# Up projections over 256 tokens as one 512-column and one 256-column matmul per chunk

## What is computed

```python
def swiglu(u, w_gate, w_up, w_down):           # layers 0 and 1, 256 tokens, hidden 2816
    return (jax.nn.silu(u @ w_gate) * (u @ w_up)) @ w_down

def sq_relu_mlp(x, w1, w2):                    # layers 2 (272 tokens) and 3 (256), hidden 4096
    h = jax.nn.relu(x @ w1)
    return (h * h) @ w2
```

## Time and profile before

| | |
|---|---|
| median of 3 runs | 1271.04 us (1270.38 to 1271.95) |
| the profiled execution: time, span | 1271.81 us, 1269.8 us |
| busy: TensorE | 1245.5 us, 98% |
| busy: VectorE, ScalarE, GpSimd | 812.0, 734.6, 365.6 us (64, 58, 29%) |
| L346, L347, L348 on `uhi`, `ulo`: matmuls | 1824 each |
| L362, L363: matmuls | 608 each |
| gu0, gu1, up3: from about | 141.8, 443.5, 1088.8 us |
| dn0, dn1, dn3: from | 264.13, 565.84, 1177.05 us |

### The profile page before, as it was taken

How to read it: one execution, slowest core, us unless ns; L and a number is a source line. 1 busy time by engine, 2 the same in 40 slices (tenths; PEclk the granted TensorE clock), 3 DMA queues, 4 the chain that set the end, 5 groups by cost and what they waited for, 6 DMA issues and landing times.

```text
span 1269.8 us, 26957 instructions
## 1 busy us (share of the span) xinstructions
PE 1245.5 (98%) x9610; PEld 1173.9 (92%) x9610; DVE 812.0 (64%) x1441; ACT 734.6 (58%) x1368; POOL 365.6 (29%) x413
## 2 busy tenths in 40 slices
PE   6999999999999999999999899999999999999998
PEld 6988999998998999998889599999999889999887
DVE  5687755566677655557799975554547766755554
ACT  6476766655455566666566864444346776544433
POOL 2011344421000144441133037770001210678100
PEclk9999999999999999999999899999999999999999
DMA  7542666667665466667655056556555443665764
GB/s 262 182 125 85 195 186 181 185 212 203 206 188 167 135 186 183 193 182 217 183 163 153 6 165 184 178 175 184 172 166 194 146 135 105 194 182 183 199 188 159
DMA packets 65761, 218.68 MB, mean 172 GB/s; under 512 B 9152, under 2 KB 13456, under 8 KB 65552
## 3 DMA queue, kind: packets, MB, share of 16 engines
q1 hardware_dynamic: 63344, 210.99, 54.9%
q10 hardware_dynamic: 2336, 6.58, 1.6%
HBM read 214.04 MB, written 1.08 MB: 169 GB/s over the span
## 4 chain that ended last, share of the span: by engine, by line
PE 76%; issue 10%; DVE 5%; POOL 4%; ACT 3%; DMA 1%; POOLq 0%; SPq 0%; ACTq 0%; DVEq 0%
PE bank L346 19%; PE bank L348 18%; PE bank L347 18%; PE bank L362 8%; PE bank L363 4%; POOL scratch L613 1%; DVE wlo L330 1%; POOL scratch L611 1%; PE bank L960 1%; PE bank L945 1%; POOL ahi_alo L615 1%; PE bank L942 1%; DVE scratch L601 1%; ACT ahi_alo L586 1%; ACT whi L325 1%
## 5 line engine op out<-in xcount | busy, mean ns | idle before, releaser
L330 DVE TENSOR_TENSOR wlo<-raw,whi 128x1024 fp32r<-128x1024 f32 (+1 forms) x391 | 479.7, 1228 | 150.1 <-ACT whi L325 148.3
L346 PE MATMUL bank<-uhi,whi 128*128 128x256 f32 (+1 forms) x1824 | 525.6, 288 | 11.5 <-DVE wlo L330 10.6
L348 PE MATMUL bank<-uhi,wlo 128*128 128x256 f32 (+1 forms) x1824 | 518.0, 284 | 0.0
L347 PE MATMUL bank<-ulo,whi 128*128 128x256 f32 (+1 forms) x1824 | 517.5, 284 | 0.0
L325 ACT ACTIVATE whi<-raw 128x1024 fp32r<-128x1024 f32 (+1 forms) x391 | 407.7, 1045 | 178.6 <-PE bank L363 102.8
L346 PEld LDWEIGHTS bank<-uhi,whi 128*128 128x128 f32 x1824 | 345.4, 189 | 19.8 <-issue 17.1
L348 PEld LDWEIGHTS bank<-uhi,wlo 128*128 128x128 f32 x1824 | 345.6, 189 | 0.0
L347 PEld LDWEIGHTS bank<-ulo,whi 128*128 128x128 f32 x1824 | 344.2, 189 | 0.5
L362 PE MATMUL bank<-ahi_alo,whi 128*128 128x512 f32 x608 | 212.4, 393 | 0.0
L363 PE MATMUL bank<-ahi_alo,wlo 128*128 128x256 f32 x608 | 170.5, 280 | 0.0
L346 PE MATMUL bank<-ahi_alo,whi 128*128 128x272 f32 (+1 forms) x560 | 162.6, 290 | 0.4 <-DVE wlo L330 0.4
(11 more groups left out here) (292 smaller groups left out, 1332.5 us busy)
## 6 DMA issues: line engine op xcount, KB each, us to landing
raw<-stream SPq DMA_DIRECT2D x391, 512.0 KB, 3.9
scratch<-decay ACTq DMA_DIRECT2D x8, 416.0 KB, 4.3
scratch<-relh ACTq DMA_DIRECT2D x8, 384.0 KB, 3.5
scratch<-scratch SPq DMA_DIRECT2D x60, 34.0 KB, 2.6
constants<-consts SPq DMA_DIRECT2D x1, 1300.0 KB, 11.0
h<-xT SPq DMA_DIRECT2D x4, 256.0 KB, 5.4
out<-h SPq DMA_DIRECT2D x8, 128.0 KB, 2.4
scratch<-scratch SPq DMA_DIRECT2D x16, 16.0 KB, 3.2
```

The source lines that it names most:

```text
L330: dve.tensor_tensor(wlo[:, s, 0:w], raw[:, s, 0:w], whi[:, s, 0:w].bitcast(F32), ALU.subtract).then_inc(w_lo, 1)
L346: pe.matmul(dst, hi, a, start=first and i == 0, stop=False)
L347: pe.matmul(dst, hi, b, start=False, stop=False)
L348: mm = pe.matmul(dst, lo, a, start=False, stop=last and i == chunks - 1)
```

## The change

`uhi` and `ulo` become halves of one tensor, so that one access pattern can stream both. In gu0, gu1 and up3 `wide_mm` takes the place of `unit_mm`. The two halves of the bank are then added before anything else: ScalarE copies the second half into a scratch tile (`half_copy`), VectorE adds the first (`half_add`), and the multiply that used to read the bank reads the sum in place. `up2` (272 tokens) stays as it was.

```diff
-        uhi = sb("uhi", DC * T, F32R)[:, :].rearrange("p (c t) -> p c t", t=T)
-        ulo = sb("ulo", DC * T, F32R)[:, :].rearrange("p (c t) -> p c t", t=T)
+        both_u = sb("uhi_ulo", 2 * DC * T, F32R)[:, :].rearrange("p (h c t) -> p h c t", h=2, t=T)
+        uhi, ulo = both_u[:, 0, :, :], both_u[:, 1, :, :]
...
+        half_t = area(V0, 2 * SEQ).rearrange("p (b t) -> p b t", b=2)
...
+                    if wide:
+                        wide_mm(pe, n0 + j, bank[(b0 + j).mod(4)][:, :], both_u, 0, DC, True, True, x)
+                    else:
+                        unit_mm(pe, n0 + j, bank[(b0 + j).mod(4)][:, 0:width(cols)], uhi, ulo, cols, x=x)
...
+        def half_copy(act, n, j, src):
+
+            act.wait_ge(w_used, (n + 1).value())
+            act.activation(half_t[:, j % 2, :], src[:, SEQ:2 * SEQ], ACT.Copy).then_inc(half_copied, 1)
+
+        def half_add(dve, u, j, src, dst):
+
+            dve.wait_ge(half_copied, (u + 1).value())
+            dve.tensor_tensor(dst, src[:, 0:SEQ], half_t[:, j % 2, :], ALU.add).then_inc(half_added, 1)
...
                     split_hi(act, n0 + (2 * j + AHEAD))
+                    half_copy(act, n0 + 2 * j, 2 * j, bank[(b0 + 2 * j).mod(4)])
                     act.wait_ge(evac, (b0 + (2 * j + 1)).value())
...
                     split_hi(act, n0 + (2 * j + 1 + AHEAD))
+                    half_copy(act, n0 + (2 * j + 1), 2 * j + 1, bank[(b0 + 2 * j + 1).mod(4)])
                     act.wait_ge(evac, (b0 + (2 * j + 2)).value())
...
-                    dve.wait_ge(w_used, (n0 + (2 * j + 1)).value())
-                    dve.tensor_tensor(gate[:, j, cols], bank[(b0 + 2 * j).mod(4)][:, 0:width(cols)],
-                                      rstd[:, 0, cols], ALU.mult).then_inc(evac, 1)
+                    half_add(dve, u, 2 * j, bank[(b0 + 2 * j).mod(4)], gate[:, j, cols])
+                    dve.wait_ge(half_added, (u + 1).value())
+                    dve.tensor_tensor(gate[:, j, cols], gate[:, j, cols], rstd[:, 0, cols], ALU.mult).then_inc(evac, 1)
                     split_lo(dve, n0 + (2 * j + AHEAD))
-                    dve.wait_ge(w_used, (n0 + (2 * j + 2)).value())
+                    half_add(dve, u + 1, 2 * j + 1, bank[(b0 + 2 * j + 1).mod(4)], mval[:, j, cols])
+                    dve.wait_ge(half_added, (u + 2).value())
                     dve.wait_ge(t_ready, (i + 1).times(2).value())
-                    dve.tensor_tensor(mval[:, j, cols], bank[(b0 + 2 * j + 1).mod(4)][:, 0:width(cols)],
-                                      tgate[:, j, cols], ALU.mult).then_inc(evac, 1)
+                    dve.tensor_tensor(mval[:, j, cols], mval[:, j, cols], tgate[:, j, cols], ALU.mult).then_inc(evac, 1)
...
+                    if u0 is not None:
+                        u = At(u0 + j, it, 4)
+                        half_add(dve, u, j, src, gate[:, j % 2, cols])
+                        dve.wait_ge(half_added, (u + 1).value())
+                        src = gate[:, j % 2, cols]
+                    dve.scalar_tensor_tensor(out=gate[:, j % 2, cols], in0=src, scalar=0.0,
+                                             in1=rstd[:, 0, cols], op0=ALU.max, op1=ALU.mult).then_inc(evac, 1)
```

More of the change, by code:

```diff
@@ L350, in unit_mm, with wide_mm @@
                 mm.then_inc(w_used, 1)
-        def wide_mm(pe, n, dst, c0, chunks, first, last, x):
+        def wide_mm(pe, n, dst, both, c0, chunks, first, last, x):
             s = n.mod(RING)
@@ L362, in wide_mm @@
                 pe.matmul(dst, hi, both[:, :, c0 + i, FIRST], start=first and i == 0, stop=end, skip_group_check=True)
-                mm = pe.matmul(dst[:, 0:SEQ], lo, ahi[:, c0 + i, FIRST], start=False, stop=end, skip_group_check=True)
+                mm = pe.matmul(dst[:, 0:SEQ], lo, both[:, 0, c0 + i, FIRST], start=False, stop=end, skip_group_check=True)
             mm.then_inc(w_used, 1)
@@ L505, in group @@
                         if wide:
-                            wide_mm(pe, n0 + (j * per + u), bank[(b0 + j).mod(4)][:, :], u * DC, min(DC, kc - u * DC), u == 0, u == per - 1,
+                            wide_mm(pe, n0 + (j * per + u), bank[(b0 + j).mod(4)][:, :], both, u * DC, min(DC, kc - u * DC), u == 0, u == per - 1,
                                     x if wait_x else None)
@@ L548, in resid_dve, with hidden_pe @@
                 split_lo(dve, At(START[name] + DC - 1 + AHEAD))
-        def hidden_pe(pe, name, cols, norm, groups):
+        def hidden_pe(pe, name, cols, norm, groups, wide=False):
             def group(it):
@@ L557, in group @@
                     pe.wait_ge(evac, (b0 + (j - 3)).value())
-                    unit_mm(pe, n0 + j, bank[(b0 + j).mod(4)][:, 0:width(cols)], uhi, ulo, cols,
-                            x=u_chunk(norm) if it is None and j == 0 else None)
+                    x = u_chunk(norm) if it is None and j == 0 else None
+                    if wide:
+                        wide_mm(pe, n0 + j, bank[(b0 + j).mod(4)][:, :], both_u, 0, DC, True, True, x)
+                    else:
+                        unit_mm(pe, n0 + j, bank[(b0 + j).mod(4)][:, 0:width(cols)], uhi, ulo, cols, x=x)
                     if it is None and j == 0:
@@ L616, in swiglu_pool, with sqrelu_pe, sqrelu_act @@
                                        hidden_at(ahi_t, At(j, it, 2), cols).bitcast(F32), ALU.subtract).then_inc(a_lo, 1)
-        def sqrelu_pe(pe, name, cols, norm):
-            hidden_pe(pe, name, cols, norm, FC2 // 4)
-        def sqrelu_act(act, name, cols):
+        def sqrelu_pe(pe, name, cols, norm, wide=False):
+            hidden_pe(pe, name, cols, norm, FC2 // 4, wide)
+        def sqrelu_act(act, name, cols, wide=False):
             with act.Fori(0, FC2 // 4) as it:
@@ L626, in sqrelu_act, with sqrelu_dve @@
                     split_hi(act, n0 + (j + AHEAD))
+                    if wide:
+                        half_copy(act, n0 + j, j, bank[(b0 + j).mod(4)])
                     act.wait_ge(evac, (b0 + (j + 1)).value())
                     act.activation(hidden_at(ahi_t, At(j, it, 4), cols), gate[:, j % 2, cols], ACT.Square).then_inc(a_hi, 1)
-        def sqrelu_dve(dve, name, cols, norm, i0):
+        def sqrelu_dve(dve, name, cols, norm, i0, u0=None):
             dve.wait_ge(rstd_ready, norm + 1)
@@ L637, in sqrelu_dve @@
                     dve.wait_ge(a_lo, (i + (-1)).value())
-                    dve.scalar_tensor_tensor(out=gate[:, j % 2, cols], in0=bank[(b0 + j).mod(4)][:, 0:width(cols)],
-                                             scalar=0.0, in1=rstd[:, 0, cols], op0=ALU.max,
-                                             op1=ALU.mult).then_inc(evac, 1)
+                    src = bank[(b0 + j).mod(4)][:, 0:width(cols)]
+                    if u0 is not None:
[5 more added lines that the diff above has]
+                                             in1=rstd[:, 0, cols], op0=ALU.max, op1=ALU.mult).then_inc(evac, 1)
                     split_lo(dve, n0 + (j + AHEAD))
@@ L2475, in _ @@
             fox_pe(pe)
-            sqrelu_pe(pe, "up3", FIRST, 7)
+            sqrelu_pe(pe, "up3", FIRST, 7, wide=True)
             resid_pe(pe, "dn3", FC2, FIRST, lambda i: (a_lo, 2 * FC1 + FC2 + i + 1), wide=True)
@@ L2503, in _ @@
             resid_act(act, link, "out3", DC, FIRST, 7, "mlp1", ahead=1)
-            sqrelu_act(act, "up3", FIRST)
+            sqrelu_act(act, "up3", FIRST, wide=True)
             resid_act(act, link, "dn3", FC2, FIRST, None, None)
@@ L2529, in _ @@
             resid_dve(dve, "out3", DC, FIRST, 7, "mlp1", ahead=1, banks=OUT_BANKS["out3"])
-            sqrelu_dve(dve, "up3", FIRST, 7, 2 * FC1 + FC2)
+            sqrelu_dve(dve, "up3", FIRST, 7, 2 * FC1 + FC2, 4 * FC1)
             resid_dve(dve, "dn3", FC2, FIRST, None, None, wide=3)
```

6 lines of the change are left out of this document (3 added, 3 removed).

## The result

The changed kernel takes 1300.2 us in the median (1299.0 to 1301.4), the kernel before 1270.7 beside it: 1.0227 times as long, with a 95% interval of 1.0214 to 1.0240. The forecast was 1299.4. The profiled execution took 1299.91 us, with a span of 1297.8.

What follows compares the result with a forecast made beforehand. TensorE, busy throughout the first SwiGLU up stage, was taken as the bound before; after, a closed chain across engines. 27.0 for gu0 and gu1 plus 1.4 for up3 gave +28.4 us, 1299.4 for the median, range 1287 to 1317.

Steps and rivals of the forecast that it cites:

- The closed chain in gu0 and gu1: SwiGLU loops: gate copy waits behind the split and the previous pair's second multiply; 6.34 us a pair against TensorE's 5.58.
- The branch through GpSimd: SwiGLU loops: last exponential through two GpSimd multiplies to the second VectorE multiply, 2.08 us, said to end just before ScalarE's.
- ScalarE's branch: SwiGLU loops: last exponential through split, up-half copy and add to the second multiply, 2.14 us, counted on the chain.
- The stages' cost: gu0 and gu1: the third unit of the following down stage starts 13.5 us later in each, together 27.0.
- up3: Third up stage: VectorE and GpSimd share a port, so 2.92 us a unit and +1.4 us; -1.6 as the other end.
- ScalarE's closed chain: up3: copy, add, relu multiply, square, split and back to copy, 2.72 us a unit, under TensorE's 2.79.
- the next relu multiply, issued before that: up3: issued before GpSimd's second instruction ends (2.64 us after the last relu multiply), it ends 0.28 later: 2.92 a unit.
- What TensorE gains: gu0, gu1 and up3: the wide matmul saves 0.10 us a pair, 6.0 us over 60 pairs if TensorE stays the bound.
- TensorE as the bound: Rival for the whole kernel: queued slack hides the chain, 1265.0 us; chance 2 in 100.
- the clock fall: Rival in the SwiGLU stages: idle TensorE drops to 1.2 GHz, half of one stage so costing 53 us; 2 in 100.

Runs made afterwards that it cites:

- gu_first: As gu_only, but ScalarE's copy of the gate half stands ahead of its weight split; 1267.59 us, 0.9972 of the kernel before.
- long_only: As gu_only, but ScalarE copies all 512 columns of the bank instead of 256, still behind the splits; 1316.6 us, 1.0359 of the kernel before.
- gu_second: As gu_only, but only the copy of the up half stands ahead of its weight split; 1298.95 us, 1.0224 of the kernel before.
- up3_first: As up3_only, but ScalarE's copy stands ahead of the weight split; 1269.98 us, 0.9991 of the kernel before.
- narrow_best: As all_best, but three 256-column matmuls a chunk in gu0, gu1 and up3; 1271.34 us, 1.0002 of the kernel before.
- all_best: The changed kernel with copies ahead of the splits in gu0, gu1 and up3, and up3's sum kept in the bank; 1265.82 us, 0.9955 of the kernel before.
- gu_only: The change in gu0 and gu1 alone, up3 as in the kernel before; 1300.0 us, 1.0221 of the kernel before.
- up3_bank: As up3_only, but the add writes its sum back into the bank, where the relu multiply reads it; 1270.13 us, 0.9989 of the kernel before.
- up3_only: The change in up3 alone, gu0 and gu1 as in the kernel before; 1273.31 us, 1.0014 of the kernel before.

## Why the prediction was right

The forecast added 13.5 + 13.5 + 1.4 = 28.4 us to the kernel; the stages measure 13.69 + 14.44 + 1.63 = 29.8. The mechanism came as laid out, with these corrections:

- **The closed chain in gu0 and gu1** (6.34 us a pair): 6.35 in gu0 and 6.39 in gu1, in the mean of 21. The steps in the rows above are 0.40 (copy to add), 0.46, 1.45, 2.16 (last exponential to second multiply), 0.56, 0.33 and 0.94, together 6.30. gu_first opened the chain and long_only lengthened it, so it is shown, not only argued.
- **The branch through GpSimd** (2.08, "ends just before"): this sentence was wrong. It takes 2.16 and ends last; ScalarE's branch, which the prediction put on the chain at 2.14, takes 2.13. The split and copy ahead of the gate add are on the chain, those ahead of the up half's add just off it. That this cost only 0.02 us a pair is luck: the two branches are nearly equal. The same mistake made the expectation of gu_second 3 us too low. The 0.08 more lie mostly in the hand-over: L619 starts 0.10 behind GpSimd's end, where L601 started 0.03 behind it in the kernel before. Why was not tried.
- **The stages' cost** (13.5 each): 13.69 and 14.44. The excess in gu1 is in one place: where the loop turns, ScalarE goes from L603 to L327 in 0.48 us instead of 0.42 (507.68 to 508.16 below), ten times, and 0.11 us more go once behind an exponential: some 0.7 us. Why a turn costs more there was not tried.
- **up3** (+1.4, 2.92 a unit): +1.63 at 2.92. The missing 0.2 is one step: behind the last relu multiply, which is held too, the low split starts 0.58 us later (1208.71 to 1209.29 in the changed kernel), not the 0.34 of an unheld one. And one sentence of the reason was not right: I had the 2.92 from VectorE and GpSimd alone. up3_first shows that it also takes ScalarE's closed chain. The step "the next relu multiply, issued before that" assumed a phase that only the closed chain brings about.
- **What TensorE gains** (0.10 us a pair, 6.0 in all), which the closed chain hid in the changed kernel: narrow_best against all_best gives 5.5. In the up stages a pair takes 5.680 and 5.587 us in these two kernels, so the price of a pair is 0.093. And the first unit of gu1 and up3, whose chunks come as the norm delivers them, takes 3.80 us from its first chunk to the second unit's in either form.
- **The rivals**: TensorE as the bound did not come. Nor did the clock fall, which stayed at 1.00 though TensorE had 6.35 - 5.59 = 0.76 us to wait in each pair.

ScalarE in gu1 of the changed kernel, at a turn of the loop:

```profile
507.68 0.42 ACT L603 ACTIVATE ahi_alo<-scratch 128x256 f32 x1 [1.08 <-DVE scratch L619]
508.16 1.06 ACT L327 ACTIVATE whi<-raw 128x1024 fp32r<-128x1024 f32 x1
```

## What to carry to other kernels

Before a drain gets a step on a second engine, write down what stands ahead of that step in the second engine's queue, and follow it back: if it leads to the drain of the round before, add up one trip round in start-to-start times and compare it with the bound's own period; the busy shares of 55 and 67% in the earlier trace rows gave no sign of it. Where two branches of the trip are nearly equal, note which one ends last and by how much: moving or shortening the other gives nothing. Where the trip is too long, look for an order before looking for less work: the step that the chain needs goes first, the prefetch behind it. Here a gain of 0.09 us a pair was lost to a single prefetch of 0.95 us in the wrong place.

## What the runs showed of the hardware beyond that

- One matmul of 512 columns and one of 256 take 0.349 us a chunk, three of 256 take 0.355, for the same 768 columns. One matmul less saves only 6 ns (all_best against narrow_best, and the earlier trace rows).
- A ScalarE copy of 256 columns out of a bank takes 0.363 us (gu_only), of 512 columns 0.578 (long_only).
- VectorE can add in place in a bank: 0.43 us in up3_bank, against 0.42 in up3_only with the sum in SBUF. The relu multiply that reads the sum from the bank takes 0.42 inside a GpSimd instruction, where with the sum in SBUF it takes 0.67.
